# Second expert table read in spans of 16 blocks by half the features, with two products per block; sums added and scores scaled on GpSimd

## The chip, the cores and the metric

The kernel runs on one core of one Trainium2 chip. The metric is the device time of a run in microseconds (us). The kernel before takes 3053.73 us, the median of three runs (3053.47 to 3054.71). Five engines matter: TensorE (PE in the profile, its weight loads PEld), VectorE (DVE), ScalarE (ACT), GpSimd (POOL) and SyncE (SP), which issues most DMAs. Each runs its own list of instructions in order and waits on semaphores for the others.

## The reference, cut to what matters

The program is two transformer blocks over 256 tokens of width 2048, in float32. The change lies in the last part of the second block, the layer of 16384 experts ("peer"):

```python
def block(args):
    xb, ib, gb = args                 # tokens, chosen experts, gates
    act = jax.nn.gelu(jnp.einsum('tkd,td->tk', expert_u[ib], xb))
    return jnp.einsum('tk,tkd->td', act * gb, expert_v[ib])
...
h = h + peer(rms_norm_2(h, ffn_norm_gain[i]), ...)
gate = jax.nn.sigmoid(rms_norm_2(h, ple_norm_gain[i]) @ w_ple_gate[i])
h = h + gate * (p[i] @ w_ple_proj[i])
```

Each token has 128 chosen experts. For 32 of the 256 tokens the kernel gathers the chosen rows of both tables. For the other 224 it computes all 16384 experts densely: scores from the first table (`expert_u`), GELU, a gate that is zero where an expert was not chosen, and a product with the second table (`expert_v`), whose sum over the experts is added to the residual.

## The kernel before, in words

Weights come in pieces of 1 MB through a ring of four slots in SBUF (class `Ring`). SyncE fills a slot when its last piece has been split. A float32 product is made of several passes in the fp32r format: ScalarE writes the rounded part of a piece (`split_hi`, L188, two instructions of 1024 elements per partition), VectorE the remainder (`split_lo`, L195, two instructions), and both parts have two halves, so that `split_hi` of piece n waits until TensorE has finished piece n-2.

The layer is one list of steps per engine, one step for each piece, called s in the code. Steps 0 to 15 are the query projection, 16 to 143 the first table (128 tiles of 128 experts), V0 = 144 to END = 272 the second table (128 blocks of 128 experts), and 16 more are the last gate (called PLE). At step s an engine splits piece s and then does whatever else the code puts at s.

*First table.* Each tile has 16 weight chunks, each with two products: the rounded weights times rounded and remainder features side by side (448 columns, L2133), and the weight remainder times the rounded features (224 columns, L2134). ScalarE copies the second half of the bank to SBUF (L2277), VectorE adds it to the first (L2397), and SyncE stores the scores in DRAM.

*Second table, before.* The scores come back in groups of 8 blocks (`s_in`, 1792 elements per partition). For each group VectorE multiplies by the norms (L2470) and ScalarE applies GELU (L2338). For each pair of blocks VectorE multiplies by the gates (L2491), ScalarE takes the rounded part (`applied_hi`, L2345) and VectorE the remainder (`applied_lo`, L2498). TensorE accumulates the sum over all 128 blocks in PSUM: 2048 features by 224 tokens fill all eight banks, two chunks of 128 features in a bank. A block takes 16 chunks with three products of 224 columns each (L2206 to L2208). At the start eight products with a zero matrix (L2205) clear the banks. After the last block VectorE adds the banks to the residual (L2506), ScalarE and VectorE make the features of the PLE gate (L2351, L2513), and its 16 pieces follow.

*Beside it.* GpSimd issues the 64 row gathers (L2113), each when VectorE has used the buffer. VectorE multiplies gathered rows of the first table by the tokens (L2451, steps in `SUM`) and adds gathered rows of the second with their weights (L2464, steps in `ADD`, 1024 elements per instruction, 64 of them).

Of the kernel before, what the change touches and what calls it, by code (L numbers as in the profile page):

```python
# [14 lines left out]
P = 128  # L15
T = 256
# [210 lines left out]
class Kernel:  # L227
# [1623 lines left out]
    def peer_stream(self):  # L1851

        a = self.a
        values = a["expert_v_2"][0].rearrange("(f h p) d -> f p h d", h=2, p=P)
# [3 lines left out]
        def source(i, j):  # L1858
            f = 4 * i + j
            if f < U:  # L1860
                return a["w_pq_2"][f].rearrange("p h k n -> p (h k) n")
            if f < V:
                return a["expert_u_2"][f - U].rearrange("p h k n -> p (h k) n")
            if f < PLE:
                return values[f - V]
            return gate(*divmod(f - PLE, 4))

        class PeerStream(Stream):
            def fill_view(self, f):
                return (2 * KD, P) if f < V else (2, D) if f < PLE else (8, BANK)  # L1870

        return PeerStream(source, (2 * KD, P), (PQ_TILES + 2 * NKEYS + KD) // 8)

    def peer(self, stream):
# [7 lines left out]
        SUM = [56, 57, *range(58, 74), *range(108, 154)]  # L1882
        DOTS = SUM[-1] + 1
        free = [s for s in range(DOTS + 4, 262) if s % 8 != 2]
        ADD = [free[k * len(free) // (2 * ROWS)] for k in range(2 * ROWS)]
        GATHERED, BACK = NKEYS - 6, [76 + 3 * j for j in range(KD // 2)]
        ROWSUM, SPREAD = 4, 6
        SCORES_AT = 60
        CURVE = lambda g: GELU + 8 * g - (5 if g == 0 else 0)
        DENSE = T - ROWS  # L1890
        GELU, PROD, SPLIT = V0 - 5, V0 - 4, V0 - 1
        LOADS = {V0 // 2 - 4: 0, V0 // 2 - 2: 1, **{V0 // 2 - 4 + 4 * g: g for g in range(2, NKEYS // 8)}}
# [13 lines left out]
        with ExitStack() as ctx:  # L1906
# [14 lines left out]
            zero = tmp("zero_weights", [P, P], F32R)  # L1921
            a_hi, a_lo = tmp("applied_hi", [P, 2, 2, DENSE], F32R), tmp("applied_lo", [P, 2, 2, DENSE], F32R)
# [31 lines left out]
            added, = sems("experts_added")  # L1954
# [109 lines left out]
            with self.block() as block:  # L2064
# [37 lines left out]
                def _(pool):  # L2102
# [3 lines left out]
                    for c in range(2 * ROWS):  # L2106
# [4 lines left out]
                        else:  # L2111
# [3 lines left out]
                            .then_inc(gathered[c % BUFS], 16)  # L2115
                    pool.wait_ge(*x_squared(KD // 2 + 3))
# [4 lines left out]
                def _(pe):  # L2121
# [65 lines left out]
                    for e in range(NKEYS):  # L2187
                        n, q = V0 + e, e // 2
                        i, j, half = at(n)
                        if e % 2 == 0:  # L2190
                            pe.wait_ge(split, q + 1)
                        ring.wait(pe, i, j, half)
                        if e == GATHERED:
                            pe.wait_ge(row_summed, 4 * ROWS)
                            for c in range(KD):
                                pe.matmul(self.bank(c // 2, ROWS, c % 2 * T), row_sum[:, c * P:(c + 1) * P], sel[:, :],  # L2196
                                          start=False, stop=False)
                        wh, wl = ring.hi[:, half, :], ring.lo[:, half, :]
                        gh, gl = a_hi[:, q % 2, e % 2, :], a_lo[:, q % 2, e % 2, :]
                        for c in (range(KD) if e > 0 else [*range(6, KD), *range(6)]):  # L2200
                            if e == 0 and c in (0, 2, 4):
                                pe.wait_ge(tile_read, V0 - 2 + c // 2)
                            out, cols = self.bank(c // 2, DENSE, c % 2 * T + ROWS), slice(c * P, (c + 1) * P)
                            if e == 0 and c % 2 == 0:
                                pe.matmul(self.bank(c // 2), zero[:, :], wh[:, 0:BANK], start=True, stop=False)  # L2205
# [811 lines left out]
```

## Time and profile before

| | |
|---|---|
| median of three runs | 3053.73 us |
| span of the profiled execution, first to last instruction | 3050.4 us |
| TensorE busy | 3008.4 us (99%) |
| VectorE busy | 1956.5 us (64%) |
| ScalarE busy | 1451.3 us (48%) |
| GpSimd busy | 169.1 us (6%) |
| granted TensorE clock, mean | 0.997 |
| moved by DMA | 690.97 MB, mean 227 GB/s |

The page gives the execution's span only; the medians of runs lie 3.3 us above it, which is what lies around the first and last instruction. A matmul's duration in the rows runs from its start until its last result is out, so matmuls overlap: how fast they follow each other is read from their start times. A granted clock of 1.00 is 2.4 GHz.

### The profile page before, as it was taken

Reading aid. Unit: us, or ns where it says so; the run is one execution under the profiler, and the core shown is the slowest. Engines: PE = TensorE matmul, PEld = TensorE weight load, DVE = VectorE, ACT = ScalarE, POOL = GpSimd, SP = SyncE. Lnnn points to the kernel's source line nnn. Section 1 sums busy time; section 2 is a strip of 40 time slices with the busy share of each in tenths; the row PEclk is TensorE's granted clock in tenths of the full one; section 3 lists DMA queues with packets and bytes.
Section 4 is the critical chain, followed back from the end, with each engine's and each line's share of the span. In section 5 each row is a group of like instructions: output and inputs, shape, how many; then the busy total and the mean of one; then the engine's idle time right before and its main releaser. Section 6 shows DMA issues by size and latency. Waiting matters only on the chain.

```text
span 3050.4 us, 46778 instructions
## 1 busy us (share of the span) xinstructions
PE 3008.4 (99%) x19141; PEld 2753.7 (90%) x19141; DVE 1956.5 (64%) x2731; ACT 1451.3 (48%) x2146; POOL 169.1 (6%) x312
## 2 busy tenths in 40 slices
PE   8999999999999999999999999999999999999999
PEld 7998778888888888878899999999999999999999
DVE  5656554444444445554558988889777777777766
ACT  4355543443444444553444475448644444444453
POOL 2000000000000002220000000000000000000000
PEclk9999999999999999999999999999999999999999
DMA  7554355565555555517667788778998888888654
GB/s 251 164 162 149 125 173 190 188 192 189 185 190 186 192 175 167 173 59 256 205 199 266 231 304 302 228 227 332 338 364 298 314 290 291 309 311 303 239 208 138
DMA packets 222011, 690.97 MB, mean 227 GB/s; under 512 B 14249, under 2 KB 95177, under 8 KB 170624
## 3 DMA queue, kind: packets, MB, share of 16 engines
q1 hardware_dynamic: 204640, 598.71, 58.5%
q0 software_dynamic: 12608, 71.73, 6.0%
q10 hardware_dynamic: 4576, 17.89, 1.6%
q8 instruction: 135, 2.21, 0.3%
q14 instruction: 52, 0.43, 0.0%
HBM read 652.61 MB, written 33.57 MB: 225 GB/s over the span
## 4 chain that ended last, share of the span: by engine, by line
PE 51%; DVE 1%; ACT 0%; ACTq 0%; issue 0%; DVEq 0%
PE banks L2133 16%; PE banks L2134 8%; PE banks L2207 8%; PE banks L2208 7%; PE banks L2206 7%; PE banks L2180 2%; PE banks L2227 1%; PE banks L2229 1%; PE banks L2228 1%; DVE weights_lo L195 0%; DVE peer_scratch L2557 0%; PE banks L2152 0%; DVE peer_features L378 0%; PE banks L2196 0%; PE banks L2169 0%; PE banks L2205 0%
## 5 line engine op out<-in xcount | busy, mean ns | idle before, releaser
L195 DVE TENSOR_TENSOR weights_lo<-weights,weights_hi 128x1024 fp32r<-128x1024 f32 (+4 forms) x1080 | 1228.2, 1179 | 807.0 <-ACT weights_hi L188 805.5
L188 ACT ACTIVATE weights_hi<-weights 128x1024 fp32r<-128x1024 f32 (+4 forms) x1080 | 1046.7, 1017 | 1411.7 <-PE banks L419 639.9
L2133 PE MATMUL banks<-peer_features,weights_hi 128*128 128x448 f32 (+1 forms) x2304 | 737.7, 377 | 2.7 <-DVE weights_lo L195 2.7
L417 PE MATMUL banks<-weights_hi,features_hi 128*128 128x512 f32 (+3 forms) x1600 | 606.0, 379 | 12.8 <-DVE weights_lo L195 9.6
L2134 PE MATMUL banks<-peer_features,weights_lo 128*128 128x224 f32 (+1 forms) x2304 | 614.6, 267 | 0.0
L419 PE MATMUL banks<-weights_hi,features_lo 128*128 128x512 f32 (+3 forms) x1600 | 600.8, 375 | 0.0
L418 PE MATMUL banks<-weights_lo,features_hi 128*128 128x512 f32 (+3 forms) x1600 | 600.7, 375 | 0.0
L2207 PE MATMUL banks<-applied_lo,weights_hi 128*128 128x224 f32 x2048 | 562.5, 275 | 0.0
L2208 PE MATMUL banks<-applied_hi,weights_lo 128*128 128x224 f32 x2048 | 562.3, 275 | 0.0
L2206 PE MATMUL banks<-applied_hi,weights_hi 128*128 128x224 f32 x2048 | 562.2, 275 | 0.0
L2133 PEld LDWEIGHTS banks<-peer_features,weights_hi 128*128 128x128 f32 x2304 | 431.9, 187 | 43.6 <-DVE weights_lo L195 3.3
L2134 PEld LDWEIGHTS banks<-peer_features,weights_lo 128*128 128x128 f32 x2304 | 438.4, 190 | 0.0
L2207 PEld LDWEIGHTS banks<-applied_lo,weights_hi 128*128 128x128 f32 x2048 | 393.2, 192 | 0.3
L2206 PEld LDWEIGHTS banks<-applied_hi,weights_hi 128*128 128x128 f32 x2048 | 393.2, 192 | 0.0
L2208 PEld LDWEIGHTS banks<-applied_hi,weights_lo 128*128 128x128 f32 x2048 | 393.2, 192 | 0.0
L417 PEld LDWEIGHTS banks<-weights_hi,features_hi 128*128 128x128 f32 x1600 | 301.2, 188 | 62.8 <-issue 11.8
L418 PEld LDWEIGHTS banks<-weights_lo,features_hi 128*128 128x128 f32 x1600 | 301.6, 189 | 45.1 <-issue 0.2
L419 PEld LDWEIGHTS banks<-weights_hi,features_lo 128*128 128x128 f32 x1600 | 301.1, 188 | 45.3
L417 PE MATMUL banks<-weights_hi,ffn_turned_hi 128*128 128x512 f32 x352 | 137.6, 391 | 0.0
L419 PE MATMUL banks<-weights_hi,ffn_turned_lo 128*128 128x512 f32 x352 | 137.3, 390 | 0.0
L418 PE MATMUL banks<-weights_lo,ffn_turned_hi 128*128 128x512 f32 x352 | 137.3, 390 | 0.0
L1301 DVE TENSOR_TENSOR ffn_turned_lo<-ffn_turned,ffn_turned_hi 128x256 fp32r<-128x256 f32 x44 | 18.7, 426 | 122.8 <-ACT ffn_turned_hi L1263 122.8
(403 smaller groups left out, 2470.0 us busy)
## 6 DMA issues: line engine op xcount, KB each, us to landing
weights<-in_expert_u SPq DMA_DIRECT2D x128, 1024.0 KB, 5.3
weights<-in_expert_v SPq DMA_DIRECT2D x128, 1024.0 KB, 5.0
weights<-in_w_ffn_gate SPq DMA_DIRECT2D x44, 1024.0 KB, 5.1
weights<-in_w_ffn_up SPq DMA_DIRECT2D x44, 1024.0 KB, 5.1
weights<-in_w_ffn_down SPq DMA_DIRECT2D x44, 1024.0 KB, 4.9
weights<-in_w_in SPq DMA_DIRECT2D x48, 900.0 KB, 4.9
weights<-in_w_out SPq DMA_DIRECT2D x32, 1024.0 KB, 5.3
weights<-in_w_in SPq DMA_DIRECT2D x24, 704.0 KB, 4.2
```

Source lines behind the costliest of these rows:

```text
L188: act.activation(hi[:, k, n], raw[:, k, n], ACT.Copy).then_inc(self.hi_ready, 1 + skip)
L195: last = dve.tensor_tensor(lo[:, k, n], raw[:, k, n], hi[:, k, n].bitcast(F32), ALU.subtract)
L417: pe.matmul(out, xh, wh, start=first, stop=False)
L418: pe.matmul(out, xh, wl, start=False, stop=False)
L419: return pe.matmul(out, xl, wh, start=False, stop=last_one)
L2133: pe.matmul(self.bank(n % 3, 2 * (T - lo)), wh[:, k, :], F[:, k, :, lo:T], start=(k == 0), stop=False)
L2134: last = pe.matmul(self.bank(n % 3, T - lo), wl[:, k, :], F[:, k, 0, lo:T], start=False, stop=(k == KD - 1))
L2180: last = pe.matmul(self.bank(3 + g % 2, P, c * P), h[:, 0, c, :], h[:, 1, c, :], start=True, stop=True)
L2206: pe.matmul(out, wh[:, cols], gh, start=False, stop=False)
L2207: pe.matmul(out, wh[:, cols], gl, start=False, stop=False)
L2208: last = pe.matmul(out, wl[:, cols], gh, start=False, stop=(e == NKEYS - 1 and c % 2 == 1))
L2227: pe.matmul(out, wh[:, k, cols], F[:, kk, 0, :], start=(kk == 0), stop=False)
```

## The change

The second table is now read as 16 spans. A span is 16 blocks by half of the features (1024), so it fills eight banks with one chunk each, and a bank has room for a second part of 224 columns. A unit of work (still one 1 MB piece, one step) is two blocks by half of the features: 8 chunks, 2 blocks, and two products each. Of the 16 steps of a group of 16 blocks the first 8 do the lower half of the features and the next 8 the upper half with the same applied weights. The pieces are now rows of 4 KB in DRAM instead of 8 KB.

After each span the banks have to be emptied: ScalarE copies the second part to SBUF (`spill_sums`), VectorE adds the first part (`leave_sums`), and GpSimd adds the result to the residual (`add_sums`). The multiplication of the scores by the norms moves from VectorE to GpSimd (`normalise`). The applied weights of nine pairs are kept, two in a buffer of their own and seven in the space of the first table's features. The zero products go. The features 0 to 7 of the PLE gate are made during the last steps of the second table.

```diff
-        values = a["expert_v_2"][0].rearrange("(f h p) d -> f p h d", h=2, p=P)
+        values = a["expert_v_2"][0].rearrange("(b p) d -> p b d", p=P)
...
-                return values[f - V]
+                g, half, pair = self.value_unit(2 * (f - V))
+                at = 16 * g + 2 * pair
+                return values[:, at:at + 4, half * (D // 2):(half + 1) * (D // 2)]
...
+                    def add_sums(pool, span):
+                        pieces = [(4 * (span % 2), 4)] if span < SPANS - 1 else [(4 + j, 1) for j in range(4)]
+                        start = 0 if span >= SPANS - 2 else ROWS
+                        for j, n in pieces:
+                            c = 2 * (j % 4)
+                            pool.wait_ge(left, CHUNKS * span + c + 2 * n)
+                            to = XT[:, j:j + n, :, start:T]
+                            pool.tensor_tensor(out=to, in0=to, in1=spill[:, c:c + 2 * n, start:T].rearrange("p (j i) t -> p j i t", i=2), op=ALU.add)\
+                                .then_inc(added, 1)
+
+                    def normalise(g):
+                        if g == 0:
+                            pool.wait_ge(spread_read, 1)
+                        pool.wait_ge(s_back[g % 2], 16 * (g // 2 + 1))
+                        pool.tensor_tensor(out=s_in[g % 2], in0=s_in[g % 2], in1=R[:, ROWS:T].unsqueeze(1).to_broadcast([P, 8, DENSE]),
+                                           op=ALU.mult).then_inc(normed, 1)
...
+                    for s in range(END + 1):
+                        if s > V0 and (s - V0) % 8 == 0:
+                            add_sums(pool, (s - V0) // 8 - 1)
+                        for g in [g for g in range(NKEYS // 8) if CURVE[g] - 1 == s]:
+                            normalise(g)
...
-                            pe.matmul(out, wh[:, cols], gh, start=False, stop=False)
-                            pe.matmul(out, wh[:, cols], gl, start=False, stop=False)
-                            last = pe.matmul(out, wl[:, cols], gh, start=False, stop=(e == NKEYS - 1 and c % 2 == 1))
...
+                            if u > 0 and pair == 0:
+                                pe.wait_ge(left, CHUNKS * (span - 1) + c + 1)
+                            cols = slice(c * P, (c + 1) * P)
+                            both = self.bank(c, 2 * T).rearrange("p (h t) -> p h t", h=2)[:, :, 0:DENSE]
+                            for e in range(2):
+                                pe.matmul(both, wh[:, e, cols], applied_pair[:, e], start=(pair == 0 and e == 0), stop=False)
+                                last = pe.matmul(self.bank(c, DENSE), wl[:, e, cols], applied_pair[:, e, 0], start=False,
+                                                 stop=(pair == 7 and e == 1))
...
+                    def spill_sums(act, span):
+                        at, cols = (ROWS, slice(T, T + DENSE)) if span < SPANS - 2 else (0, slice(DENSE, 2 * DENSE + ROWS))
+                        if span > 0:
+                            act.wait_ge(added, span)
...
+                            act.activation(spill[:, c, at:T], self.psum[:, c * BANK + cols.start:c * BANK + cols.stop], ACT.Copy)\
+                                .then_inc(spilled, 1)
...
+                    def leave_sums(dve, span):
+                        for c in range(CHUNKS):
+                            dve.wait_ge(spilled, CHUNKS * span + c + 1)
+                            dve.tensor_tensor(spill[:, c, ROWS:T], self.bank(c, DENSE), spill[:, c, ROWS:T], ALU.add).then_inc(left, 1)
...
-                            dve.tensor_tensor(s_in[g % 2], s_in[g % 2], R[:, ROWS:T].unsqueeze(1).to_broadcast([P, 8, DENSE]), ALU.mult)\
-                                .then_inc(normed, 1)
```

The steps at which things are done are now lists. Seen from the first step of a group of 16 blocks, rounded parts and remainders of the next group's pairs (`SPLIT`) are made at steps 9, 10, 12, 13, 15, 17, 18, 20, the gate products (`PROD`) at 7, 9, 11, 12, 13, 15, 17, 19, and GELU (`CURVE`) at 6 and 11, each with `normalise` of the same scores one step ahead. Spans end at 8 and 16.

TensorE inside the second table, before (the names are the applied weights' rounded part and remainder, and the piece's):

```order
L2206 MATMUL banks<-applied_hi,weights_hi7 128x224
L2207 MATMUL banks<-applied_lo,weights_hi7 128x224
L2208 MATMUL banks<-applied_hi,weights_lo7 128x224
L2206 MATMUL banks<-applied_hi,weights_hi7 128x224
L2207 MATMUL banks<-applied_lo,weights_hi7 128x224
L2208 MATMUL banks<-applied_hi,weights_lo7 128x224
```

And after, in the same place, for the same amount of work (two chunks of one block):

```order
L2261 MATMUL banks<-applied_parts,weights_hi7 128x2x224
L2262 MATMUL banks<-applied_parts,weights_lo7 128x224
L2261 MATMUL banks<-applied_parts,weights_hi7 128x2x224
L2262 MATMUL banks<-applied_parts,weights_lo7 128x224
L2261 MATMUL banks<-applied_parts,weights_hi7 128x2x224
L2262 MATMUL banks<-applied_parts,weights_lo7 128x224
L2261 MATMUL banks<-applied_parts,weights_hi7 128x2x224
L2262 MATMUL banks<-applied_parts,weights_lo7 128x224
```

Two products with the rounded weights have become one of twice the columns; the first four rows after are what the six before were.

VectorE around a group's scores in the second table, before (`normed` holds the scores, `peer_rstd` the norms, `row_tokens` the gathered rows' sum):

```order
L195 TENSOR_TENSOR weights_lo<-weights,weights_hi 128x1024 x2
L2498 TENSOR_TENSOR applied_lo<-normed,applied_hi 128x448
L195 TENSOR_TENSOR weights_lo<-weights,weights_hi 128x1024 x2
L2470 TENSOR_TENSOR normed<-normed,peer_rstd 128x1792
L2491 TENSOR_TENSOR normed<-normed,peer_scratch 128x448
L195 TENSOR_TENSOR weights_lo<-weights,weights_hi 128x1024 x2
L2464 SCALAR_TENSOR_TENSOR row_tokens<-expert_rows,row_gates,row_tokens 128x1024
```

And after, around the end of a span:

```order
L195 TENSOR_TENSOR weights_lo<-weights,weights_hi 128x1024 x2
L2494 TENSOR_TENSOR peer_scratch<-banks,peer_scratch 128x224 x8
L195 TENSOR_TENSOR weights_lo<-weights,weights_hi 128x1024 x2
L2565 TENSOR_TENSOR peer_features<-normed,peer_features 128x2x224
L2574 TENSOR_TENSOR normed<-normed,peer_scratch 128x448
L195 TENSOR_TENSOR weights_lo<-weights,weights_hi 128x1024 x2
L2545 SCALAR_TENSOR_TENSOR row_tokens<-expert_rows,row_gates,row_tokens 128x1024
L2565 TENSOR_TENSOR peer_features<-normed,peer_features 128x2x224
```

The instruction of 1792 elements is gone from VectorE, and eight of 224 elements stand at each span's end; the remainder of the applied weights is now L2565 and the gate product L2574.

GpSimd over some 40 steps of the second table, after (before, its list there is 32 gathers and nothing else):

```order
L2148 TENSOR_TENSOR residual<-residual,peer_scratch 128x4x2x224 [waits peer_sums_left]
L2155 TENSOR_TENSOR normed<-normed,peer_rstd 128x1792 [waits peer_scores_back1]
L2137 DMA expert_rows<-in_expert_v,attention_statistics 128x2048 [waits peer_rows_summed] x2
L2148 TENSOR_TENSOR residual<-residual,peer_scratch 128x4x2x224 [waits peer_sums_left]
L2137 DMA expert_rows<-in_expert_v,attention_statistics 128x2048 [waits peer_rows_summed]
L2155 TENSOR_TENSOR normed<-normed,peer_rstd 128x1792 [waits peer_scores_back0]
L2137 DMA expert_rows<-in_expert_v,attention_statistics 128x2048 [waits peer_rows_summed] x2
```

Two kinds of instructions with 1792 elements and two SBUF operands now stand between the gathers.

## Rows read from the trace of the kernel before

**Rows 1.** The page, the span; and its chain, by line
```profile
span 3050.4 us, 46778 instructions
...
PE banks L2133 16%; PE banks L2134 8%; PE banks L2207 8%; PE banks L2208 7%; PE banks L2206 7%; PE banks L2180 2%; PE banks L2227 1%; PE banks L2229 1%; PE banks L2228 1%; DVE weights_lo L195 0%; DVE peer_scratch L2557 0%; PE banks L2152 0%; DVE peer_features L378 0%; PE banks L2196 0%; PE banks L2169 0%; PE banks L2205 0%
```

**Rows 2.** Busy time by stage: first table's second part, its end, second table
```profile
core 0: us, PE busy (x) PEld busy (x) DVE busy (x) ACT busy (x) POOL busy (x), PEclk, DMA share, GB/s
1765.00:2260.80 495.80, 495.80 (x3307) 475.29 (x3306) 420.72 (x797) 305.32 (x561) 29.05 (x27) 1.00 0.84 300
2211.00:2260.80 49.80, 49.80 (x320) 47.49 (x319) 39.94 (x54) 23.12 (x32) 4.85 (x5) 1.00 1.02 394
2260.90:2952.40 691.50, 691.50 (x6186) 691.13 (x6184) 487.22 (x488) 312.44 (x340) 36.68 (x34) 1.00 0.80 285
```

**Rows 3.** TensorE in order of time, first table: start us, duration us, instruction
```profile
2219.85 0.37 PE L2133 MATMUL banks<-peer_features,weights_hi 128*128 128x448 f32 x1
...
2222.98 0.37 PE L2133 MATMUL banks<-peer_features,weights_hi 128*128 128x448 f32 x1
```

**Rows 4.** The same in the second table
```profile
2299.92 0.28 PE L2206 MATMUL banks<-applied_hi,weights_hi 128*128 128x224 f32 x1
...
2302.94 0.28 PE L2206 MATMUL banks<-applied_hi,weights_hi 128*128 128x224 f32 x1
```

**Rows 5.** Waits in the second table: us in total, times, longest
```profile
ACT weights_hi L188 <- PE banks L2208: 364.8, 123, 6.5
DVE weights_lo L195 <- ACT weights_hi L188: 198.3, 126, 6.0
```

**Rows 6.** Groups of VectorE and ScalarE by form, second table
```profile
L195 DVE TENSOR_TENSOR weights_lo<-weights,weights_hi 128x1024 fp32r<-128x1024 f32 x256 | 302.2, 1222 | 198.3 <-ACT weights_hi L188 198.3
L2464 DVE SCALAR_TENSOR_TENSOR row_tokens<-expert_rows,row_gates,row_tokens 128x1024 f32<-128x1024 f32 x62 | 79.3, 1280 | 0.0
L2498 DVE TENSOR_TENSOR applied_lo<-normed,applied_hi 128x448 fp32r<-128x448 f32 x63 | 39.0, 619 | 3.4 <-ACT applied_hi L2345 3.4
L2470 DVE TENSOR_TENSOR normed<-normed,peer_rstd 128x1792 f32<-128x1792 f32 x15 | 30.3, 2019 | 0.0
L2338 ACT ACTIVATE normed<-normed 128x1792 f32<-128x1792 f32 x15 | 25.3, 1688 | 0.0
L2451 DVE CUSTOM_DVE_ANT_0 expert_rows<-expert_rows,row_tokens 128x1024 f32<-128x1024 f32 x10 | 12.2, 1219 | 0.0
```

**Rows 7.** The page's group of ScalarE's rounded weight parts
```profile
L188 ACT ACTIVATE weights_hi<-weights 128x1024 fp32r<-128x1024 f32 (+4 forms) x1080 | 1046.7, 1017 | 1411.7 <-PE banks L419 639.9
```

**Rows 8.** VectorE's additions of two halves in the first table, min/median/max ns
```profile
L2397 DVE TENSOR_TENSOR peer_scores<-banks,peer_rest x128: 377/384/386, 1566.4 to 2264.5; 128x224 f32<-128x224 f32 x128
```

**Rows 9.** VectorE in order of time: two instructions back to back
```profile
1299.11 0.41 DVE L1477 TENSOR_TENSOR rope_parts<-mla_q_turned,sin 128x256 f32<-128x256 f32 x1
1299.44 0.42 DVE L1478 TENSOR_TENSOR rope_parts<-mla_q_turned,sin 128x256 f32<-128x256 f32 x1
```

**Rows 10.** GpSimd's two-operand instructions, min/median/max ns
```profile
L656 POOL TENSOR_TENSOR normed<-normed x6: 320/322/834, 1191.2 to 1195.9; 128x64 f32<-128x64 f32 x6
L1347 POOL TENSOR_TENSOR pool_band<-pool_band,identity x8: 462/686/913, 1282.2 to 1286.9; 128x128 f32<-128x128 f32 x8
```

**Rows 11.** VectorE's line 1004, min/median/max ns, and one of it beside GpSimd
```profile
L1004 DVE TENSOR_TENSOR projections<-projections x2: 1217/1220/1224, 285.8 to 290.1; 128x1024 f32<-128x1024 f32 x2
279.32 1.52 POOL L1119 TENSOR_SCALAR_AFFINE_SELECT nsa_q<-nsa_q 128x1024 f32<-128x1024 f32 x1 [47.94 <-ACT nsa_q L938]
279.92 2.00 DVE L1004 TENSOR_TENSOR projections<-projections,normed 128x1024 f32<-128x1024 f32 x1
```

**Rows 12.** GpSimd beside VectorE in order of time
```profile
1193.89 0.83 POOL L656 TENSOR_TENSOR normed<-normed 128x64 f32<-128x64 f32 x1
1192.75 1.80 DVE L195 TENSOR_TENSOR weights_lo<-weights,weights_hi 128x704 fp32r<-128x704 f32 x2 [2.10 <-ACT weights_hi L188]
```

**Rows 13.** Waits from 1280 to 1290 us, where L1347 runs
```profile
PE banks L417 <- DVE weights_lo L195: 1.3, 2, 0.8
```

**Rows 14.** DMA issues: count, KB each, median us to landing
```profile
weights<-in_expert_v SPq DMA_DIRECT2D x128, 1024.0 KB, 5.0
weights<-in_w_ple_gate SPq DMA_DIRECT2D x16, 1024.0 KB, 5.2
normed<-expert_scores SPq DMA_DIRECT2D x16, 896.0 KB, 8.5
```

More of the change, by code:

```diff
@@ L2105, in _, with gather @@
                     self.rstd_of_tiles(pool, D)
-                    for c in range(2 * ROWS):
+                    def gather(c):
                         if c % 8 == 0 and c < ROWS:
@@ L2186, in _ @@
                     pe.wait_ge(scores_read, NT * PARTS)
-                    for e in range(NKEYS):
-                        n, q = V0 + e, e // 2
+                    for u in range(NKEYS):
+                        n, (g, part, pair) = V0 + u, self.value_unit(u)
                         i, j, half = at(n)
-                        if e % 2 == 0:
-                            pe.wait_ge(split, q + 1)
+                        span = 2 * g + part
+                        if part == 0:
+                            pe.wait_ge(split, 8 * g + pair + 1)
@@ L2192, in _ @@
                         ring.wait(pe, i, j, half)
-                        if e == GATHERED:
+                        if g == NKEYS // 16 - 1 and pair == 6:
                             pe.wait_ge(row_summed, 4 * ROWS)
[L2195 to L2205, printed above, removed]
-                            pe.matmul(out, wh[:, cols], gh, start=False, stop=False)
-                            pe.matmul(out, wh[:, cols], gl, start=False, stop=False)
-                            last = pe.matmul(out, wl[:, cols], gh, start=False, stop=(e == NKEYS - 1 and c % 2 == 1))
-                            if e == NKEYS - 1 and c % 2 == 1 and c < KD - 1:
+                            for c in range(CHUNKS):
+                                d = (CHUNKS * part + c) * P
+                                pe.matmul(self.bank(c, ROWS, DENSE), row_sum[:, d:d + P], sel[:, :], start=False, stop=False)
@@ new lines, in _ @@
+                        wh, wl = [w[:, half, :].rearrange("p (e d) -> p e d", e=2) for w in (ring.hi, ring.lo)]
+                        applied_pair = parts_of_pair(8 * g + pair)
+                        for c in (range(CHUNKS) if u > 0 else [*range(3, CHUNKS), *range(3)]):
+                            if u == 0 and c < 3:
+                                pe.wait_ge(tile_read, V0 - 2 + c)
+                            if u > 0 and pair == 0:
[6 more added lines that the diff above has]
+                                                 stop=(pair == 7 and e == 1))
+                            if pair == 7 and c < CHUNKS - 1:
@@ L2482, in _ @@
                                 one_hots(g, 2 * place_in_order + g % 2)
-                        q = (s - PROD) // 2
-                        if (s - PROD) % 2 == 0 and 0 <= q < NKEYS // 2:
+                        if s > V0 and (s - V0) % 8 == 0:
+                            leave_sums(dve, (s - V0) // 8 - 1)
+                        for q in [q for q in range(PAIRS) if SPLIT[q] == s]:
+                            dve.wait_ge(halved, q + 1)
+                            if free_after(q) is not None:
+                                dve.wait_ge(ring.used, piece_done(free_after(q)))
+                            hi, lo = [parts_of_pair(q)[:, :, h, :] for h in range(2)]
+                            dve.tensor_tensor(lo, s_in[q // 4 % 2][:, 2 * (q % 4):2 * (q % 4) + 2, :], hi.bitcast(F32),
+                                              ALU.subtract).then_inc(split, 1)
+                        for q in [q for q in range(PAIRS) if PROD[q] == s]:
                             g = q // 4
```

144 lines of the change are left out of this document (76 added, 68 removed).

## The prediction, made before the changed kernel ran

> **What bounds the kernel now.** I read the page's chain first: the chain by line [rows 1] is TensorE lines from end to end, the second table's L2206 to L2208 among them at 22% together. Then the busy time by stage: in the second table TensorE is busy 691.50 of 691.50 us at clock 1.00, VectorE 487.22, ScalarE 312.44, GpSimd 36.68, and DMA has a share of 0.80 [rows 2]. Then the waits there: ScalarE waits 364.8 us for TensorE, VectorE 198.3 us for ScalarE, and TensorE for nobody [rows 5]. So the stage lasts as long as its products, and VectorE has about 200 us to spare. How fast products follow one another is in the start times: one of 448 columns and one of 224 start every (2222.98-2219.85)/10 = 0.313 us [rows 3]; 27 products of 224 columns take 302.94-299.92 = 3.02 us, 0.112 us each [rows 4].
>
> **The change part by part.**
>
> *Products.* Before: 128 x 16 x 3 = 6144 products x 0.112 = 687 us, and the measured 691.5 leaves 4.5 for the eight of the zero matrix and the gathered rows' sum. After: 128 steps x 8 chunks x 2 blocks = 2048 couples of 448 + 224 columns x 0.313 = 641 us. Of the 4.5 I keep 3.6, since the rows' sum has as many products as before. So 644.6 us and a gain of 46.9. A step now lasts 5.01 us instead of 5.4. The couple's price is the first table's, where the moving side is the strided one; here the PSUM side has a gap of 32 columns. I take no cost for that; the other end is that a product of 2 x 224 costs as two, 3 x 0.112 = 0.336 a couple, 688 us, and the gain is gone.
>
> *Emptying the banks.* After each span eight copies on ScalarE and eight additions on VectorE. The addition is L2397's, 0.384 us [rows 8]; back to back, 256-wide ones start 0.33 us apart [rows 9], so eight of 224 take about 2.4 us. ScalarE's rounded part of the piece takes two of 1.02 [rows 7], so it starts copying 2.1 us after the last step but one is done. Chunk 0 is ready on VectorE by about 4 us, and TensorE asks for it at 5.0; chunk 7 is finished by TensorE at 5.0, emptied by 5.9 and asked for at 5.0 + 7 x 0.63 = 9.4. Hidden, zero; if it were not, 15 spans x at most 1 us.
>
> *VectorE's sum.* Splits 302.2, row additions 79.3 + 2 first ones (about 1.5), gate products and remainders 39 each, row products about 14, [rows 6], emptying 15 x 2.4 = 36, features 4; the 30.3 of L2470 go. That makes 515 us of 644.6, 80% busy, against 70% before. The first table's second part runs at 420.72/495.80 = 85% without a wait of TensorE [rows 2]. By itself this costs nothing.
>
> *GpSimd's new instructions.* 16 of 1792 elements for the scores and 15 for the sums (and four short ones after the stage). 64 elements take 0.320 us and 128 take 0.462 [rows 10]: 2.22 ns an element and 0.18 to start, so 4.15 us each. Their own time would be hidden: 31 x 4.15 = 129 us on an engine with 37 of 691 busy. But see what they do to VectorE. L1004 with two SBUF operands takes 1.22 us; the one that starts at 279.92 takes 2.00. GpSimd's L1119 runs from 279.32 to 280.84 [rows 11], 0.92 us into it, and 0.92 + 1.1 is the 2.00: VectorE stood still until GpSimd was done. The reverse shows too: L656, 0.32 alone, took 0.83 and ended 0.17 us behind VectorE's L195 [rows 12]; and while eight of L1347 ran, TensorE waited 1.3 us for VectorE's remainders [rows 13], which it does nowhere in the second table. So each new instruction stops VectorE's two-operand work for up to 4.15 us, and splits, remainders, gate products and row additions are all such.
>
> The Trainium skill has this as a rule (page "SBUF — State Buffer", section "Who interferes with whom"): a VectorE instruction with two SBUF inputs and a GpSimd one that reads SBUF exclude each other for the whole instruction, whoever starts first. The rows above agree. The section "Elementwise — side-by-side cycle accounting" of "GPSIMD Engine Reference" gives 4497 ns for 2048 elements; scaled, an estimate of 3.9 us for 1792, which would make the loss below some 6% of it smaller.
>
> *What a stop costs.* From the moment TensorE finishes piece s-2: ScalarE needs 2.1 us for the rounded part, VectorE's second half ends 1.2 us later, at 3.4; TensorE wants it at 5.0. If VectorE is still busy b us with the previous step, the piece is ready at b + 2.36, if that is later. TensorE is stopped when b plus stop is over about 2.6.
> - The sums' addition is released right behind the emptying, at b = 0.8 of the next step: 0.8 + 4.15 + 2.36 = 7.3, less 5.0, is 2.4 (a tenth for the signal). 15 x 2.4 = 36 us.
> - Scores at step 10 of a group (7 of them) come right behind that: VectorE still has the backlog (7.3 + 1.9 of other work - 5.0 = 4.2), so 4.2 + 4.15 + 2.36 = 10.7 against a step stretched to 7.4, 3.4 each. 24 us.
> - Scores at step 5 (7 of them) fall into light steps: half are absorbed. VectorE finishes its split at 3.4, is stopped until 7.55, is 2.55 or (with a row addition, 7 steps in 10) 3.8 late, and the next piece comes at 4.9 or 6.1 of 5.0: 0.9 on average. 6 us.
> - The two before the second table, in the first one's busy steps: 1 each, 2 us.
>
> Together 68 us. Queued behind these on GpSimd are the gathers; their three buffers allow some 25 us. GELU on ScalarE waits for the scores; they land about 8.5 us after their issue [rows 14], two steps before.
>
> The ends of this term: nothing, if all stops fall into VectorE's idle time (515 + 29 x 4.15 = 635 us, which just fits into 644.6), and 31 x 3.4 = 105 us if each costs what the worst does.
>
> *DMA.* Same bytes in 7% less time: share 0.80 becomes 0.86. The last 50 us of the first table run at 1.02 and 394 GB/s with TensorE busy 49.80 of 49.80 [rows 2]. Rows of 2 KB (PLE gate) land in 5.2 us, of 8 KB in 5.0 [rows 14]. Zero; at the other end a piece is late now and then, 5 us.
>
> *The end.* Half of the PLE features are made under the second table, and only four short sums follow; TensorE did not wait there before, so nothing is gained; bound 2 us either way.
>
> **The sum.** 3050.4 + 3.3 around it = 3053.7; - 46.9 + 68 = 3074.8. I say 3074.
>
> **The rivals.**
> 1. *The stops are mostly absorbed.* For it: VectorE's free 130 us in the stage, and light steps (4 to 7, 14) that take a whole stop. Against: the additions come right behind the emptying, the heaviest step. At 1.2 us a stop, 37 us: 3044, faster. It decides from 47/31 = 1.5 us a stop: below it the kernel is faster.
> 2. *No stop is seen.* GpSimd gets its operands between VectorE's, or shares with it. Against: rows 11 to 13. 3053.7 - 46.9 = 3007.
> 3. *The wide product costs as two* because its result goes to two places of a bank. Nothing in the rows has such a result. Products alone 688 + 3.5, equal to before; steps of 5.4 absorb more of the stops, 40 us stay: 3093.
> 4. *ScalarE is stopped by late scores.* At steps 6 and 11 GELU waits for GpSimd, which itself waits for VectorE; the next rounded part comes late, and VectorE idles. 14 x 1.5 us on top of the forecast: 3096.
>
> **How the numbers follow.** Forecast 0.50, own range 3058 to 3092; rival 1 0.22 (3025 to 3058), rival 2 0.13, rivals 3 and 4 0.15 together. 0.2% (6 us) is about what a measurement of this kernel tells from no change, so faster means under 3047.6 and slower over 3059.8. Faster: 0.13 + most of rival 1 (0.16) + a little of the forecast's tail = 0.32; same 0.12; slower 0.56. Range 3012 to 3098: it leaves out most of rival 2 and the far end of the slow ones.
>
> **What the changed profile would show.** Couples 0.313 us apart in the second table (else rival 3). GpSimd's two new lines at 4 us or more, 31 of 1792 elements. VectorE's splits with a mean well over 1.22 us in the stage, some over 4: the stops. TensorE's idle time with VectorE's L195 as releaser, near 68 us, mostly in the two steps after a span's end. If L195 keeps 1222 ns, rival 2. If ScalarE waits long for `normed` at GELU, rival 4. The forecast is wrong if TensorE's waits for L195 sum up to less than 47 us, or if the stage's products do not take 641.

## The result, and the profile after

The changed kernel takes 3103.78 us, the median of four runs (3100.71 to 3112.64), against 3053.60 of the kernel before (3053.02 to 3054.71). The ratio is 1.0169, with a 95% interval of 1.0153 to 1.0185: slower by 1.7%. The forecast was 3074 with a range to 3098. The sign was right; the time lies 6 us outside the range.

The page's head of the kernel after, beside [rows 1]:

```profile
span 3099.0 us, 42961 instructions
PE 2991.4 (97%) x17085; PEld 2699.7 (87%) x17085; DVE 2063.4 (67%) x2834; ACT 1490.6 (48%) x2274; POOL 312.1 (10%) x347
...
PE 46%; DVE 4%; issue 2%; ACT 1%; ACTq 0%; DVEq 0%
```

VectorE now has 4% of the chain, against 1% before: TensorE waited for it. The next step is to find where. Stretches of the kernel before, then of the kernel after (the columns are those of [rows 2]):

```profile
0.00:2190.00 2190.00, 2152.39 (x11729) 1901.69 (x11730) 1342.94 (x2085) 1058.44 (x1699) 123.76 (x269) 1.00 0.62 206
2190.00:3002.00 812.00, 811.84 (x7047) 807.97 (x7046) 585.44 (x610) 376.78 (x427) 45.36 (x43) 1.00 0.81 290
```

```profile
0.00:2190.00 2190.00, 2151.59 (x11730) 1901.05 (x11731) 1343.22 (x2084) 1058.48 (x1699) 122.97 (x269) 1.00 0.62 206
2190.00:3002.00 812.00, 747.02 (x4585) 706.03 (x4584) 654.16 (x676) 388.09 (x517) 182.20 (x73) 0.96 0.80 276
```

Up to 2190 us the two are the same. Behind it two things differ. TensorE is idle for 812 - 747.02 = 65.0 us, and its granted clock is 0.96 instead of 1.00: some 32 us of full clock are missing. The waits of that stretch (engine and line, whom it waited for, us in total, times, longest):

```profile
ACT weights_hi L188 <- PE banks L2262: 318.3, 111, 6.1
...
DVE weights_lo L195 <- ACT weights_hi L188: 157.8, 117, 4.4
...
PE banks L2261 <- DVE weights_lo L195: 59.8, 21, 6.1
```

In [rows 5] TensorE waited for nobody. Here it waits 21 times for VectorE's remainders in the second table, up to 6.1 us, and twice more at the end of the first (5.2 us together). Groups of the same stretch, with the busy time, the mean ns of one, and the idle time before them:

```profile
L195 DVE TENSOR_TENSOR weights_lo<-weights,weights_hi 128x1024 fp32r<-128x1024 f32 x284 | 424.4, 1535 | 157.8 <-ACT weights_hi L188 157.8
...
L2155 POOL TENSOR_TENSOR normed<-normed,peer_rstd 128x1792 f32<-128x1792 f32 x16 | 74.9, 4682 | 38.4 <-DMA normed<-expert_scores 38.4
...
L2148 POOL TENSOR_TENSOR residual<-residual,peer_scratch 128x1792 f32<-128x1792 f32 x14 | 56.9, 4063 | 139.1 <-DVE peer_scratch L2494 139.1
...
L2494 DVE TENSOR_TENSOR peer_scratch<-banks,peer_scratch 128x224 f32<-128x224 f32 x127 | 39.2, 384 | 0.0
```

The mean of a split has risen from 1222 to 1535 ns [rows 6]. A sum of GpSimd takes 4.06 us, against 4.15 estimated. Emptying a chunk costs the 0.384 us that was taken from [rows 8].

How a stop looks when a sum and a group of scores follow each other. First GpSimd, then VectorE, then TensorE (start, duration, line, and in brackets the idle time before and its releaser):

```profile
2495.20 4.07 POOL L2148 TENSOR_TENSOR residual<-residual,peer_scratch 128x1792 f32<-128x1792 f32 x1 [4.94 <-DVE peer_scratch L2494]
2499.22 4.95 POOL L2155 TENSOR_TENSOR normed<-normed,peer_rstd 128x1792 f32<-128x1792 f32 x1
```

```profile
2492.64 2.47 DVE L2494 TENSOR_TENSOR peer_scratch<-banks,peer_scratch 128x224 f32<-128x224 f32 x8
2495.57 9.68 DVE L195 TENSOR_TENSOR weights_lo<-weights,weights_hi 128x1024 fp32r<-128x1024 f32 x2 [0.45 <-ACT weights_hi L188]
```

```profile
2505.30 0.74 PE L2261 MATMUL banks<-peer_features,weights_hi 128*128 128x448 f32 x1 [6.09 <-DVE weights_lo L195]
...
2506.61 0.60 PE L2261 MATMUL banks<-peer_features,weights_hi 128*128 128x448 f32 x1
...
2507.20 0.60 PE L2261 MATMUL banks<-peer_features,weights_hi 128*128 128x448 f32 x1
...
2509.30 0.37 PE L2261 MATMUL banks<-peer_features,weights_hi 128*128 128x448 f32 x1
...
2509.61 0.38 PE L2261 MATMUL banks<-peer_features,weights_hi 128*128 128x448 f32 x1
```

GpSimd's sum starts as soon as the eight emptying additions end, at 2495.20. VectorE's two halves of a split take 9.68 us instead of 2.35, until GpSimd has finished at 2504.17. TensorE stands for 6.09 us. And when it starts again, couples follow each other at 0.59 us (2506.61 to 2507.20), later at 0.31 (2509.30 to 2509.61). Windows of 1 us of the same moment show why:

```profile
2501.00:2502.00 1.00, 0.00 (x0) 0.00 (x0) 1.00 (x1) 0.31 (x1) 1.00 (x1) 1.00 1.07 396
2502.00:2503.00 1.00, 0.00 (x0) 0.00 (x0) 1.00 (x1) 0.00 (x0) 1.00 (x1) 0.58 0.81 324
2503.00:2504.00 1.00, 0.00 (x0) 0.00 (x0) 1.00 (x1) 0.00 (x0) 1.00 (x1) 0.50 0.33 135
...
2506.00:2507.00 1.00, 1.00 (x5) 0.93 (x4) 1.00 (x2) 0.58 (x1) 0.00 (x0) 0.50 0.68 115
...
2508.00:2509.00 1.00, 1.00 (x5) 0.91 (x5) 1.00 (x2) 0.00 (x0) 0.00 (x0) 0.51 0.95 356
2509.00:2510.00 1.00, 1.00 (x8) 0.96 (x8) 1.00 (x2) 0.00 (x0) 0.00 (x0) 1.00 0.97 340
```

During the wait the granted clock falls from 2.4 to 1.2 GHz (1.00 to 0.50), and it stays at 1.2 GHz for more than 3 us of work behind the wait. The forecast had no term for that.

For every kernel below I added up, over 81 windows of 10 us from 2190 to 3000 us, the idle time of TensorE and the missing clock (1 less the granted clock, times 10 us). Part of the missing clock falls into the waits themselves, where it costs nothing that the waits don't cost already; the last column, from windows of 0.5 us, has only what is missing while TensorE works. Before 2190 us the kernels differ by at most 2.5 us of idle time and 5.2 of clock.

| kernel | median, us | ratio to before, 95% | TensorE idle, us | clock missing, us | of it while TensorE works, us |
|---|---|---|---|---|---|
| before | 3053.6 | | 0.2 | 0.0 | 0.0 |
| after | 3103.78 | 1.0169 (1.0153 to 1.0185) | 65.0 | 32.4 | 25.4 |
| e1, scores on VectorE | 3069.38 | 1.0055 (1.0038 to 1.0072) | 35.9 | 23.8 | 23.8 |
| e2, sums on VectorE | 3043.42 | 0.9961 (0.9948 to 0.9973) | 23.8 | 10.2 | 10.1 |
| e3, both on VectorE | 3008.62 | 0.9855 (0.9838 to 0.9871) | 0.0 | 0.0 | 0.0 |
| e4, quarters | 3074.52 | 1.0071 (1.0054 to 1.0088) | 44.6 | 13.6 | 12.1 |
| e7, quarters apart | 3067.16 | 1.0042 (1.0025 to 1.0059) | 38.8 | 13.6 | 12.2 |
| e6, GpSimd only writes | 3008.23 | 0.9849 (0.9832 to 0.9865) | 1.0 | 0.0 | 0.0 |
| e8, before with scores on GpSimd | 3103.03 | 1.0164 (1.0147 to 1.0181) | 27.8 | 18.8 | 18.7 |
| e9, narrow filler products | 3105.60 | 1.0161 (1.0144 to 1.0178) | 25.2 | 28.9 | 25.8 |
| e10, wide filler products | 3089.01 | 1.0114 (1.0097 to 1.0130) | 20.3 | 5.1 | 5.1 |
| e11, sums in light steps | 3028.31 | 0.9916 (0.9899 to 0.9932) | 15.5 | 3.4 | 3.4 |

Idle time and the last column account for most of the times: e3 at 3008.6, with 65.0 + 25.4 added, gives 3099.0 for the kernel after, whose profiled execution took 3100.71, and with e1's 35.9 + 23.8 it gives 3068.3, where 3069.38 was measured. In e4 and e7, with 39 and 37 waits of TensorE, 9 and 8 us are left over. Part of this is how idle time is counted: a product of 224 columns is busy for 0.27 us in the rows where the next can start after 0.11 (e4, 2318.85 and 2318.96), so a wait costs some 0.16 us more than its idle time (an estimate).

### The profile page after: what moved, and what is told of

The parts are those of the page before. It is cut to its first block, busy times and chain, and to the rows that moved or that the text cites. A ratio compares the mean times of both kernels' runs of the same rounds, so it can differ in the third digit from the quotient of the medians.

```text
span 3099.0 us, 42961 instructions
## 1 busy us (share of the span) xinstructions
PE 2991.4 (97%) x17085; PEld 2699.7 (87%) x17085; DVE 2063.4 (67%) x2834; ACT 1490.6 (48%) x2274; POOL 312.1 (10%) x347
## 4 chain that ended last, share of the span: by engine, by line
PE 46%; DVE 4%; issue 2%; ACT 1%; ACTq 0%; DVEq 0%
PE banks L2185 15%; PE banks L2261 12%; PE banks L2186 8%; PE banks L2262 6%; DVE weights_lo L195 3%; PE banks L2232 2%; PE banks L2282 1%; PE banks L2284 1%; PE banks L2283 1%; ACT weights_hi L188 1%; DVE row_tokens L2545 0%; PE banks L2204 0%; DVE peer_features L378 0%; DVE peer_features L2565 0%; PE banks L2221 0%
## 5 line engine op out<-in xcount | busy, mean ns | idle before, releaser
L195 DVE TENSOR_TENSOR weights_lo<-weights,weights_hi 128x1024 fp32r<-128x1024 f32 (+4 forms) x1080 | 1318.9, 1263 | 755.8 <-ACT weights_hi L188 754.3
L2261 PE MATMUL banks<-peer_features,weights_hi 128*128 128x448 f32 x1568 | 512.2, 384 | 52.5 <-DVE weights_lo L195 52.5
L2185 PEld LDWEIGHTS banks<-peer_features,weights_hi 128*128 128x128 f32 x2304 | 432.7, 188 | 49.5 <-DVE weights_lo L195 9.0
L2186 PEld LDWEIGHTS banks<-peer_features,weights_lo 128*128 128x128 f32 x2304 | 439.2, 191 | 0.0
L2262 PE MATMUL banks<-peer_features,weights_lo 128*128 128x224 f32 x1568 | 421.6, 269 | 0.0
L2261 PEld LDWEIGHTS banks<-peer_features,weights_hi 128*128 128x128 f32 x1568 | 303.4, 193 | 80.7 <-DVE weights_lo L195 35.2
L2262 PEld LDWEIGHTS banks<-peer_features,weights_lo 128*128 128x128 f32 x1568 | 308.2, 197 | 0.0
L2261 PE MATMUL banks<-applied_parts,weights_hi 128*128 128x448 f32 x480 | 157.8, 383 | 7.3 <-DVE weights_lo L195 7.3
L2262 PE MATMUL banks<-applied_parts,weights_lo 128*128 128x224 f32 x480 | 130.6, 272 | 0.0
L268 POOL TENSOR_SCALAR statistics<-statistics 128x2 f32<-128x2 f32 (+3 forms) x16 | 6.9, 429 | 1048.9 <-DVE statistics L395 864.5
```

The source lines that it names most:

```text
L195: last = dve.tensor_tensor(lo[:, k, n], raw[:, k, n], hi[:, k, n].bitcast(F32), ALU.subtract)
L2185: pe.matmul(self.bank(n % 3, 2 * (T - lo)), wh[:, k, :], F[:, k, :, lo:T], start=(k == 0), stop=False)
L2186: last = pe.matmul(self.bank(n % 3, T - lo), wl[:, k, :], F[:, k, 0, lo:T], start=False, stop=(k == KD - 1))
L2261: pe.matmul(both, wh[:, e, cols], applied_pair[:, e], start=(pair == 0 and e == 0), stop=False)
L2262: last = pe.matmul(self.bank(c, DENSE), wl[:, e, cols], applied_pair[:, e, 0], start=False, stop=(pair == 7 and e == 1))
```

## Experiments

My theory: GpSimd's two new instructions read SBUF and stop VectorE's two-operand work for as long as they run, and the stops reach TensorE as waits, which cost their length and then clock. The main rival: the new product loop itself, or the emptying of the banks, is what costs.

### One or both of the new GpSimd instructions back on VectorE: e1, e2, e3

```diff
 # e1 and e3: on VectorE at step CURVE[g] - 1, GpSimd's normalise(g) gone
+dve.tensor_tensor(s_in[g % 2], s_in[g % 2], R[:, ROWS:T]..., ALU.mult)
 # e2 and e3: on VectorE at V0 + 8 * (span + 1) + 6 (span 14: + 1), GpSimd's add_sums gone
+dve.tensor_tensor(to, to, spill[:, c:c + 2 * n, start:T]..., ALU.add)
```

e1: 

> The changed kernel, but the scores are scaled by the norms on VectorE again (same steps); the sums stay on GpSimd. Theory 1 (a GpSimd instruction with SBUF operands stops VectorE's two-operand work for its whole length, TensorE runs dry, and its granted clock then falls to half for some us): the 15 stops of the sums' additions remain, each worth about 2.5 us of waiting and 1.7 us of clock, so 3007 + 15 x 4.2 = 3070, between 3058 and 3080. Rival 2 (emptying the banks at the end of each span is what stops TensorE, whoever adds): about 3100, as the changed kernel. Rival 3 (scores that come late from GpSimd stop ScalarE): near 3010.

e2: 

> The changed kernel, but the sums are added on VectorE, six steps behind a span's end; the scores stay on GpSimd. Theory 1: the 16 stops of the scores remain, half of them in light steps and none on top of another: 16 x about 2 us with the clock, 3007 + 32 = 3039, between 3025 and 3055. Rival 2: still about 3100, since the banks are emptied as before. Rival 3: still about 3100.

e3: 

> The changed kernel with both back on VectorE: the spans and the two products per block alone, and nothing but gathers on GpSimd. Theory 1: no stop, VectorE at 515 + 30 + 30 = 575 of 645 us (89%), so the products set the time: 3007, between 3005 and 3018; clock 1.00 in the second table. Rival 2: 3090 or more. If VectorE's load itself is too much for single steps, 3020 to 3040.

Measured: 3069.38, 3043.42 and 3008.62 us, within 5 us of what the theory said each time. (In e2 and e3 the sums also come later, six steps behind a span's end.) In e3 (stretches as above, the second one most of the second table; then the split in it):

```profile
2190.00:3002.00 812.00, 812.00 (x5367) 779.11 (x5366) 676.17 (x782) 430.04 (x575) 55.37 (x43) 1.00 0.84 297
2261.00:2902.00 641.00, 641.00 (x4096) 611.84 (x4095) 549.21 (x625) 344.72 (x461) 47.50 (x35) 1.00 0.88 308
```

```profile
L195 DVE TENSOR_TENSOR weights_lo<-weights,weights_hi 128x1024 fp32r<-128x1024 f32 x256 | 302.1, 1222 | 90.9 <-ACT weights_hi L188 89.9
```

4096 products, 2048 couples, in 641.00 us, which is 0.313 each. TensorE has no idle time, the split is back at 1222 ns, and VectorE is 86% busy without harm. So the new product loop gives 43.8 us (3052.46 - 3008.62; 39 to 49 by the interval) where 46.9 were forecast, and the GpSimd instructions cost 95 us (3103.8 - 3008.6). That refutes the main rival. e3 beats both kernels.

### Does GpSimd's reading do it, or its being busy: e6

```diff
-pool.tensor_tensor(out=to, in0=to, in1=..., op=...)
+pool.memset(to, 0.5)          # three times, at both places
```

The kernel leaves out the scaling of the scores and the adding of the sums.

e6: 

> The changed kernel with each of GpSimd's two-operand instructions of 1792 elements replaced by three memsets of the same 1792 elements, in the same places of its list: the scaling and the sums are left out. GpSimd is about as long busy but reads nothing. Theory 1, with the stop laid to GpSimd's reads: no stops, 3007 to 3015, TensorE's waits for VectorE under 5 us. If anything that GpSimd runs in SBUF stops VectorE: 3060 to 3100. Rival 3 (GpSimd as such is late, with scores and gathers): about 3100.

```profile
2190.00:3002.00 812.00, 811.01 (x5358) 777.82 (x5357) 614.27 (x746) 430.14 (x573) 199.51 (x148) 1.00 0.84 296
```

3008.23 us, as e3. GpSimd is busy for 199.51 us, more than the 182.20 of the kernel after, and TensorE hardly ever waits. Busy time of GpSimd costs nothing; its reading of two operands does. (With the reads the arithmetic went as well; no run separates those two.)

### The scores alone, on the kernel before: e8

```diff
 # the kernel before, steps of 5.4 us, three products a chunk
-dve.tensor_tensor(s_in[g % 2], s_in[g % 2], R[:, ROWS:T]..., ALU.mult)
+pool.tensor_tensor(out=s_in[g % 2], in0=s_in[g % 2], in1=R[:, ROWS:T]..., op=ALU.mult)
```

e8: 

> The kernel before with only the scaling of the scores moved to GpSimd (16 instructions of 1792 elements), no spans, three products per block, steps of 5.4 us. Theory 1 holds without the rest of the change: 14 stops in the second table, each 0.5 to 1.5 us of TensorE's waiting beyond the slack of 3 us, and some clock: 3053 + 20 = 3073, between 3058 and 3085. Rival 2 (it is the spans' ends): 3053, no change.

```profile
PE banks L2223 <- DVE weights_lo L195: 25.2, 15, 2.1
PE banks L2150 <- DVE weights_lo L195: 2.5, 1, 2.5
```

3103.03 us, 30 more than expected. Moving 16 multiplications to GpSimd, with only the order of its gathers changed beside them, costs 49 us: 27.8 of waits and 18.8 of clock. The mechanism needs nothing of the new loop. The size was wrong on both counts. The waits are 1.7 us each instead of 0.5 to 1.5, and the clock took almost as much as all that was forecast for both. Why the waits are so long can be read from VectorE (GpSimd's multiplication runs from 2498.70 to 2502.74):

```profile
2499.13 5.84 DVE L195 TENSOR_TENSOR weights_lo<-weights,weights_hi 128x1024 fp32r<-128x1024 f32 x2 [1.27 <-ACT weights_hi L188]
```

In twelve of the sixteen cases the multiplication begins just before a split, and the split's first half alone takes 4.68 to 4.73 us. The stop falls on the split at almost its whole length.

### Shorter instructions: e4 and e7

```diff
 # e4: four instructions of 448 elements for one of 1792, at both places
+for i in range(0, n, small):
+    last = pool.tensor_tensor(out=to, in0=to, in1=..., op=ALU.add)
 # e7: the same, each quarter waiting for the one before
+    self.pool_chain.on(pool)(last)
```

e4: 

> The changed kernel with each GpSimd instruction of 1792 elements cut into four of 448. GpSimd works longer (4 x 1.17 = 4.7 us instead of 4.15), but VectorE can go between. Theory 1: a stop is at most 1.2 us, less than the slack of 2.6 us, but VectorE alternates with GpSimd, so a piece's remainders are late by up to 2.4 us: most waits of TensorE and the clock's falls go, 3007 to 3035. If the length of one instruction does not matter, only the sum: about 3100 or a little more.

e7: 

> As the quarters (each GpSimd instruction of 1792 elements in four of 448), but each quarter waits on a semaphore for the one before, so that GpSimd's list is empty for a moment between them. In the quarters run VectorE's L195 once took 5.89 us beside four quarters in a row: it did not get between. If a waiting VectorE instruction goes first as soon as GpSimd has nothing queued: stops of at most 1.2 us each, alternating, 3020 to 3050. If the sum of GpSimd's time is all that counts: 3070 to 3085, as the quarters run (3074.5).

3074.52 and 3067.16 us. e4 missed both of its expectations and e7 lies just below its second one. In e4, a sum and then a group of scores, GpSimd first, then VectorE, then TensorE:

```profile
2315.41 7.45 POOL L2151 TENSOR_TENSOR residual<-residual,peer_scratch 128x448 f32<-128x448 f32 x4 [9.62 <-DVE peer_scratch L2501]
...
2324.20 4.41 POOL L2161 TENSOR_TENSOR normed<-normed,peer_rstd 128x448 f32<-128x448 f32 x4
```

```profile
2315.76 3.99 DVE L195 TENSOR_TENSOR weights_lo<-weights,weights_hi 128x1024 fp32r<-128x1024 f32 x2 [0.43 <-ACT weights_hi L188]
...
2323.81 7.02 DVE L195 TENSOR_TENSOR weights_lo<-weights,weights_hi 128x1024 fp32r<-128x1024 f32 x2
```

```profile
2318.85 0.27 PE L2269 MATMUL banks<-applied_parts,weights_lo 128*128 128x224 f32 x1
2318.96 0.38 PE L2268 MATMUL banks<-applied_parts,weights_hi 128*128 128x448 f32 x1
...
2319.80 0.47 PE L2268 MATMUL banks<-applied_parts,weights_hi 128*128 128x448 f32 x1 [0.36 <-DVE weights_lo L195]
...
2330.88 0.74 PE L2268 MATMUL banks<-peer_features,weights_hi 128*128 128x448 f32 x1 [5.78 <-DVE weights_lo L195]
```

At 2315 the two engines take turns: four quarters stretch to 7.45 us and two halves of a split to 3.99, and TensorE waits 0.36 us, where a single sum in one piece cost 2.4. At 2323 they don't: the split lasts 7.02 us, its first half (5.89 us) spans all four quarters of 4.41, and TensorE waits 5.78. So quarters help where the engines take turns and not where they don't, and GELU on ScalarE now waits 41.1 us for the scores (3.0 in the kernel after), which made some of TensorE's shorter waits (about 4 us of the 44.6): the split starts late because ScalarE's rounded part comes late. That fits a gain of 29 us and not 70 or more. Which of the two happens, and why, stays open.

### Where the stop falls: e11

```diff
 # scores on VectorE as in e1; sums on GpSimd, held back to 6 steps behind the span's end
+pool.wait_ge(ring.lo_ready, ...)   # VectorE's split of that step
 add_sums(pool, ...)
```

e11: 

> As the run with the scores on VectorE (3069), but GpSimd's additions of the sums are held back until VectorE has split the piece six steps behind the span's end, where VectorE has least other work; the instructions are the same. Theory 1 with the backlog rule: the stop begins with VectorE 3.4 us into a step with at most one row addition, so the next piece is 0.9 us late on average instead of 2.4, and the clock falls less: 3007 + 15 x 1.5 = 3030, between 3015 and 3045. If each stop costs the same wherever it falls: 3065 to 3072.

3028.31 us, against 3069.38 of e1, which has the same instructions on the same engines. The waits of TensorE in the second table, in e1 and then in e11:

```profile
PE banks L2259 <- DVE weights_lo L195: 35.9, 15, 2.8
```

```profile
PE banks L2262 <- DVE weights_lo L195: 15.5, 13, 2.8
```

A wait is now 15.5/13 = 1.2 us instead of 35.9/15 = 2.4, and the missing clock falls from 23.8 to 3.4. How it comes about is in the rows. VectorE in e1, behind the eight emptying additions, with GpSimd's sum of 4.05 us beside it:

```profile
2480.63 5.90 DVE L195 TENSOR_TENSOR weights_lo<-weights,weights_hi 128x1024 fp32r<-128x1024 f32 x2 [0.45 <-ACT weights_hi L188]
```

And in e11, GpSimd first:

```profile
2498.63 5.06 POOL L2148 TENSOR_TENSOR residual<-residual,peer_scratch 128x1792 f32<-128x1792 f32 x1 [11.72 <-DVE weights_lo L195]
```

```profile
2498.47 1.28 DVE L2546 SCALAR_TENSOR_TENSOR row_tokens<-expert_rows,row_gates,row_tokens 128x1024 f32<-128x1024 f32 x1
2501.21 4.71 DVE L195 TENSOR_TENSOR weights_lo<-weights,weights_hi 128x1024 fp32r<-128x1024 f32 x2 [1.46 <-ACT weights_hi L188]
```

The sum starts beside VectorE's row addition and takes 1 us longer than in e1, as do twelve of the fifteen, so here GpSimd waited for VectorE. Another part of it falls into the 1.46 us in which VectorE has nothing to do. The two halves of the split take 4.71 us instead of 5.90.

### The clock: e9 and e10

Both put products that are not used or add nothing ahead of TensorE's wait behind a span's end, so that it works while it would wait.

```diff
 # e9: 32 columns each
+for filler in range(9 if u % 16 == 1 else 18):
+    pe.matmul(self.bank(0, 32, 480), self.ident[:, :], self.ones[:, 0:32], start=False, stop=False)
 # e10: a zero matrix times 448 columns
+for filler in range(11 if u % 16 == 1 else 21):
+    pe.matmul(..., zero[:, :], parts_of_pair(8 * g + pair)[:, 0], start=False, stop=False)
```

e9: 

> The changed kernel with products that nobody reads (32 columns, into a corner of bank 0) put ahead of TensorE's wait in the second step of each span: about 2.0 us of them where the wait was 2.42 us, and 4.0 us where it was 6.1 us at most. They fill time in which TensorE stands. If the falls of the granted clock (32 us lost in the changed kernel's second table) come from TensorE standing: the clock's loss falls to 10 us or less, the time to 3075 to 3090. If the clock falls for another reason: 3100 to 3110, the fillers adding up to 6 us where a wait was shorter.

e10: 

> As the filler run, but the products that fill TensorE's wait in the second step of each span are of full width: zero weights times 448 columns of the applied weights, added to bank 0 (they change nothing), 11 or 21 of them, 2.0 or 3.9 us. The fillers of 32 columns left the clock's loss at 28.9 us. If the clock falls because few columns go through TensorE around the stop, whether it stands or runs narrow products: the loss falls to 12 us or less, and the time to 3075 to 3090. If it falls for another reason, such as the wait's end itself: the loss stays near 30 us and the time at 3100 to 3108.

A stop in e9 and the one at the same place in e10, windows of 10 us (in the first of them the kernel after has 4.70 us busy and a clock of 0.66):

```profile
2500.00:2510.00 10.00, 7.84 (x60) 7.58 (x59) 10.00 (x4) 3.19 (x4) 7.75 (x2) 0.88 0.87 305
2510.00:2520.00 10.00, 10.00 (x52) 9.38 (x52) 6.31 (x8) 3.41 (x4) 0.00 (x0) 0.78 0.66 211
```

```profile
2500.00:2510.00 10.00, 9.80 (x61) 9.06 (x60) 10.00 (x8) 4.18 (x4) 2.97 (x1) 1.00 0.71 253
2510.00:2520.00 10.00, 10.00 (x66) 9.54 (x65) 7.57 (x9) 4.95 (x6) 1.12 (x1) 1.00 0.90 320
```

With narrow fillers TensorE counts as busy, but the clock still falls: 28.9 us are missing, and the time is no better (3105.60). That is e9's second expectation; the first, that standing alone brings the clock down, failed. With wide fillers the clock stays at 1.00 here, 5.1 us are missing in all, and the time is 3089.01, 15 less than the kernel after, as e10's first expectation had it. The two differ in more than width: e9's are plain float32 and not fp32r, and they leave 14.9 us of idle time at the fifteen places, e10's 4.2. No run separates these. From the first filler to the next product of the loop, the fifteen places of e10 take 55.9 us, where the waits of the kernel after took 51.1. So some 20 us of clock come back while TensorE works (25.4 less 5.1), 5 go to fillers that last longer than the waits, and 15 are left. The clock's loss is a cost of its own: most of it can be taken away while the stop of VectorE stays.

## Why the prediction was wrong in its size

By its own steps:

- *Products*: right. Forecast 641 us for 2048 couples, measured 641.00 in e3. Here a result with a gap of 32 columns in a bank cost nothing. The gain of the loop as a whole was 43.8 us, 3 less than forecast, within the interval.
- *Emptying the banks*: right. No wait of TensorE in e3, which still empties them; 0.384 us an addition.
- *VectorE's sum*: right. In e3 it is 86% busy with both added works on it, and TensorE never waits for it.
- *GpSimd's duration*: 4.15 forecast, 4.06 measured for a sum; for scores 4.68 in the mean, up to 5.13, since they in turn wait for VectorE (the 4.95 above begins inside VectorE's split).
- *What a stop costs*: right as a mechanism, and near in total, 68 us forecast and 65.0 idle, but partly by terms that offset each other. Sums that no scores followed at once: 2.4 forecast, 2.28 to 2.43 measured in ten of eleven (the last, of 2048 elements, 2.82). Sums and scores together: 2.4 + 3.4 = 5.8 forecast for seven. Four waits are of 6.08 to 6.11; at the other three the scores began 1.0 to 4.8 us after the sum's end and cost only 1.92, 0.28 and 1.52. Together the second stops cost 18 us, not 24. Scores at step 5: 0.9 forecast, 0 to 2.5 measured, 5 in all. The two in the first table: 1 each forecast, 2.5 and 2.7 measured. e1, e2, e3 and e6 show the cause. The rule of the Trainium skill that the prediction cited (page "SBUF — State Buffer", section "Who interferes with whom") agrees with the whole-instruction stop of the 9.68 us row, and with e6, whose writes stop nothing.
- *DMA, the end*: right. Share 0.88 at full speed in e3, and no wait.
- *The sum*: this is the step that failed. It priced a wait of TensorE at the wait's length and had no term for the granted clock. While TensorE worked, 25.4 us of clock were missing on top. With it the sum is 3074.8 + 25.4 - 3.0 for the waits' difference (68 against 65.0) = 3097.2. The profiled execution took 3100.71 and the four lie between 3100.71 and 3112.64, so 3.5 us are left to the first and 6.6 to the median. By the estimate of 0.16 us more for each of 23 waits, 3.7 of them are waits too; no run shows it by itself. The rows of before could not show the clock term, as TensorE never waits in the second table [rows 2, 5].

Rival 1 failed at its own bound: the 31 instructions cost 65.0/31 = 2.1 us each, over its 1.5, before clock. Rival 2 is refuted by the same waits, and rival 3 by e3's couples. For rival 4, ScalarE's GELU waited for GpSimd 3.0 us in total in the kernel after, not 21; it appeared only with the quarters (41.1 us in e4, 47.0 in e7).

Still open: when quarters take turns with VectorE, and why four of the seven groups of scores at step 5 cost TensorE nothing while the others cost 0.97 to 2.51 us.

## What to carry to other kernels

An instruction moved to an idle engine is free only if it does not stop the engine that feeds the bound. Here 31 GpSimd instructions that read SBUF, 136 us of busy time, turned 44 us of gain (e3) into 50 us of loss. Keep them off GpSimd while VectorE's two-operand work feeds TensorE, or release them in its lightest step (e11 against e1: 41 us). And price a wait of TensorE at its length plus the clock: 0.4 us more for each us of wait in the kernel after, 0.7 in e1 and e8, 0.2 in e11, whose waits are short. Clock that is missing during a wait is not counted again.

## What the runs showed of the hardware

- Waits of 2.4 us every 40 to 50 us already cost clock: e1 has no longer one than 2.8 us and loses 23.8 us. In e11, with 1.2 us in the mean, it is 3.4.
- Fillers of 32 columns left 28.9 us of clock missing, fillers of 448 columns 5.1, where either takes away some 40 to 45 us of the idle time. Their format and the idle time that they leave differ too.
- Splitting GpSimd's instructions in four does not always let VectorE through. In one place the two halves of a split took 3.99 us beside four quarters, in another 7.02.
- The stop works both ways: a sum that starts beside VectorE's row addition takes 5.05 us instead of 4.06 (e11).
- GpSimd's fills run beside VectorE without a stop: 199.51 us busy, and TensorE idle for 1.0.
